# Two more u tiles in each head of the PEER ranking, and more gathered dots beside them

## The chip, the cores and the metric

One core of one Trainium2 chip runs the whole kernel. The metric is device microseconds for one execution; lower is better. Three runs of the kernel before gave 2048.4, 2052.14 and 2053.71 us, median 2052.14.

## The reference, cut to what matters

The kernel computes a hybrid encoder block for 512 positions of width 1024 (16 meta tokens and 512 frames go in; the last layer norm is on 512). Input norm, one combined projection, a sparse attention branch, a recurrent branch, output projection and norm come first and are not touched. The change lies in the last part, a product-key retrieval of single-neuron experts:

```python
q = (xf @ wq).reshape(n, 8, 2, 128)
s = einsum('nhpd,hpkd->nhpk', q, subkeys)          # 8 heads, 2 halves, 128 keys
s_top, i_top = top_k(s, 16)
best_s, best_j = top_k(all 16 x 16 sums of pairs, 16)
expert = key1 * 128 + key2;  gate = softmax(best_s)
h = einsum('nd,nhkd->nhk', xb, u[expert])
coef = gate * gelu(h)
out = einsum('nhk,nhkd->nd', coef, v[expert])      # u, v: 16384 x 1024
```

Each position picks 8 x 16 = 128 of 16384 experts.

## The kernel before, in words

**Two ways through the experts.** For 384 positions (`DENSE`) the kernel computes densely: all 16384 experts in 128 tiles of 128, each a *u tile* (u times the activations, then gelu) and a *sum* (weighted coefficients times v). For the first 128 positions it gathers: GpSimd issues an indirect DMA for each of the 128 picks of u rows and then of v rows (`gather_rows`, L1542), and VectorE does a dot with the u row (`dot_rows`, L1552) or adds the weighted v row (`add_rows`, L1561). Eight slots (`GATHER_RING`) hold gathered rows; the gather of number n waits until dot n - 8 is done.

**A weight tile.** Weights are split into a high and a low part in float32r. The SyncE queue loads a 512 KB tile into `w_staged`, ScalarE writes its high part (L1833, L1868), GpSimd (L1804) or from the lots on VectorE (L2173) writes the low part as the difference. TensorE multiplies 16 times with the high part (L1934) and then, after a wait for the low part, 8 times with the low part (L1938). Four slots hold split weights, so ScalarE and the low part run at most three to four tiles ahead of TensorE. ScalarE applies the gelu to the finished tile (L1839) and sends it to HBM (`parked_gelu`, a *parked* tile, 192 KB), from where it is loaded in the sums.

**The stages.**
- *Ranking*, 8 heads. Each head has 6 weight tiles: two query tiles (512 positions), then four u tiles (384 positions); the scores against the subkeys (L1948) stand ahead of the second u tile. ScalarE copies the scores behind that second u tile's gelu (L1860), and VectorE ranks them (`rank`, L2065 to L2119): maxima, indexes and replacements on 128 keys, a cast of the indexes (L2085), sums of pairs (L2086), the same on 256 candidates, then the lookup of the picked keys (L2092 to L2114) and `pick_index` (L2119). Behind the rank of head h VectorE does the dots of head h - 1 (`DOTS_A_HEAD`, 3). GpSimd makes the low parts in order; behind the last one of head h + 1 it waits for the index of head h and issues that head's gathers, in one block.
- *Between*, 16 u tiles. VectorE makes the gate softmax; ScalarE does its exponential behind tile 9 of them, and TensorE transposes picks and gates ahead of tile 12 (`GATES_AT`), for which it waits.
- *Lots*, 24 of 16 positions each. The gates are spread into dense form by one-hot matmuls (L1992), with two u tiles, two gathers and two dots in each lot. SyncE stores 1 MB for each lot, and issues two weight loads with it.
- *Behind the lots*, 6 u tiles with one dot each. GpSimd issues the gathers freely from here on, and already in the lots.
- *Sums*, 128 of them, L2019. For the first 102 (`PARKED`) the gelu is loaded; for the other 26 (`FRESH`) a u tile is computed two experts ahead. VectorE weighs with the gates (L2200), splits the coefficients (L2204), makes the low parts, and does the rest of the dots and adds in step (`used_by`): 1.1 for each parked expert, then about 3 for each fresh one.

Each engine's order is written out by hand in its own block; semaphores count tiles. The host lays `stream` out in the order in which the tiles are used.

Of the kernel before, what the change touches and what calls it, by code (L numbers as in the profile page):

```python
# [41 lines left out]
EXPERT_KEYS, PEER_HEADS, PEER_TOPK = 128, 8, 16  # L42
LOT = 16
PICKS = PEER_HEADS * PEER_TOPK

DENSE = SEQ - P
LOTS = DENSE // LOT
BETWEEN = 16
PARKED = 4 * PEER_HEADS + BETWEEN + 2 * LOTS + 6
GATHER_RING = 8  # L50
MARK, FILL, LOW = -3.4e38, -3.3e38, -1.0e30

# [64 lines left out]
def build(nc, a, out):  # L117

    with ExitStack() as ctx:
# [20 lines left out]
        gates_dram = nc.dram_tensor("branch_gates", [2 * KD, P, SEQ], F32, kind="Internal").ap()  # L140
        parked = nc.dram_tensor("parked_gelu", [PARKED, P, DENSE], F32, kind="Internal").ap()

# [1422 lines left out]
def peer(nc, a, g, out):  # L1565
# [3 lines left out]
    h_tok, gathering, eps = g["h_tok"], g["gathering"], g["eps"]  # L1569
    NP = PEER_HEADS * PEER_TOPK  # L1570
    K = PEER_TOPK
    PER_HEAD = 6
    QUERIES = 2 * PEER_HEADS
    TOPK_TILES = PEER_HEADS * PER_HEAD
    FIRST_LOT = TOPK_TILES + BETWEEN
# [6 lines left out]
    RING = 4  # L1582
    BY_POOL = FIRST_LOT
    DEEP = 2 * RING
    LOOP, COEFS, HLS = 8, 4, 3
    TILES_D = DENSE // P
    FRESH = EXPERT_KEYS - PARKED
    LEAD = 2

    V_AT, U_AT, s = {}, {}, QUERIES + PARKED  # L1590
    for k in range(EXPERT_KEYS):
        if k + LEAD < EXPERT_KEYS and k + LEAD >= PARKED:
# [3 lines left out]
        s += 1  # L1596
    STREAMED = s

    BEHIND = PARKED - (4 * PEER_HEADS + BETWEEN + 2 * LOTS)
    DOTS_A_HEAD, DOTS_A_LOT, DOTS_BEHIND = 3, 2, 1  # L1600
    IN_LOTS = DOTS_A_HEAD * (PEER_HEADS - 1)
    used_behind = [IN_LOTS + DOTS_A_LOT * LOTS + DOTS_BEHIND * (n + 1) for n in range(BEHIND)]
    EARLY = used_behind[-1]
    A_PARKED = 1.1
    BEFORE_FRESH = EARLY + int(A_PARKED * PARKED)
    used_by = [EARLY + int(A_PARKED * (k + 1)) if k < PARKED else
               min(2 * PICKS, BEFORE_FRESH + -(-(2 * PICKS - BEFORE_FRESH) * (k + 1 - PARKED) // (FRESH - HLS)))
               for k in range(EXPERT_KEYS)]
    DOTTED = next(k for k in range(EXPERT_KEYS) if used_by[k] >= PICKS)
    used_by[DOTTED] = PICKS  # L1610

    def expert_of(s):

        return s // PER_HEAD * (PER_HEAD - 2) + (s % PER_HEAD - 2) if s < TOPK_TILES else s - QUERIES

    def place_of(s):

# [29 lines left out]
    with ExitStack() as ctx:  # L1647
# [53 lines left out]
        w_high, w_low, late_low = sem("w_high"), sem("w_low"), sem("late_low")  # L1701
        tile_done, gelu_made = sem("tile_done"), sem("gelu_made")
# [17 lines left out]
        tile_bank = lambda n, is_query: n % 2 if is_query else 2 + n % 2  # L1720
# [98 lines left out]
        def _(act):  # L1819
# [8 lines left out]
            def high(s, j, landings, free=True):  # L1828

                act.wait_ge(landed[j % RING], landings * 16)  # L1830
                if free:
                    act.wait_ge(tile_done, s - 2)
                nc.scalar.activation(w_hl[:, j % RING, 0, :], staged[:, j % RING, :], ACT.Copy).then_inc(w_high, 1)  # L1833

            def gelu(s, n, m, turn, bank):

                act.wait_ge(tile_done, s + 2)
                act.wait_ge(act_parked[m % 2], turn * 16)
                nc.scalar.activation(act_out[:, m % 2, 0:DENSE], ps[:, bank, 0:DENSE], ACT.Gelu).then_inc(gelu_made, 1)  # L1839
                act.wait_ge(gelu_made, n + 3)  # L1840
                nc.scalar.dma_start(parked[n], act_out[:, m % 2, 0:DENSE]).then_inc(act_parked[m % 2], 16)
# [4 lines left out]
            with act.Fori(0, PEER_HEADS // 2) as i:  # L1846
                for j in range(2 * PER_HEAD):
                    r, m = j // PER_HEAD, j % PER_HEAD
                    high(i * (2 * PER_HEAD) + (j + 3), j + 3, i * 3 + ((j + 3) // RING + 1))
                    if m < 2:  # L1850
                        act.wait_ge(tile_done, i * (2 * PER_HEAD) + (j + 2))
                        nc.scalar.activation(qT[:, m, :], ps[:, tile_bank(m, True), :], ACT.Copy).then_inc(q_copied, 1)
                        continue
                    n = 4 * r + m - 2
                    gelu(i * (2 * PER_HEAD) + j, i * 8 + n, n, i * 4 + (n // 2 + 1), tile_bank(n, False))
                    if m == 3:
                        act.wait_ge(topped, i * 2 + (r + 1))
                        for x in range(2):
                            act.wait_ge(s_done, i * 4 + (2 * r + x + 1))
                            nc.scalar.activation(s_head[:, r, x], ps[:, 4 + 2 * r + x, :].rearrange("p (t k) -> p t k", t=NT),  # L1860
                                                 ACT.Copy).then_inc(s_copied, 1)
# [25 lines left out]
            for n in range(LOTS):  # L1887
                if n >= 2:
                    act.wait_ge(lot_stored[n % 2], 16 * (n // 2))
                s = FIRST_LOT + TILES_A_LOT * n  # L1890
# [32 lines left out]
        def _(pe):  # L1923
            pe.sem_inc(tile_done, 1)

            def tile(s, j, bank, width, low, before):

                pe.wait_ge(w_high, s + 1)
                for x in before:
                    pe.wait_ge(*x)  # L1930
                lo = SEQ - width
                for k in range(KD):
                    for part in range(2):
                        nc.tensor.matmul(ps[:, bank, 0:width], w_hl[:, j % RING, 0, P * k:P * (k + 1)],  # L1934
                                         h_hl[:, part, k, lo:SEQ], start=(k == 0 and part == 0), stop=False)
# [19 lines left out]
            with pe.Fori(0, PEER_HEADS // 2) as i:  # L1955
                for j in range(2 * PER_HEAD):
                    r, m = j // PER_HEAD, j % PER_HEAD
                    s = i * (2 * PER_HEAD) + j
                    if m < 2:
                        tile(s, j, tile_bank(m, True), SEQ, (w_low, s + 1), [(q_copied, i * 4 + (2 * r + m + 1))])  # L1960
                        continue
                    if m == 3:
                        scores(i, r)
                    n = 4 * r + m - 2
                    tile(s, j, tile_bank(n, False), DENSE, (w_low, s + 1), [(gelu_made, i * 8 + (n + 1))])

            low_of = lambda s: (w_low, s + 1) if s < BY_POOL else (late_low, s - BY_POOL + 1)

# [293 lines left out]
def lay_out(v):  # L2262

    w = v["w_in"][0]
    A = HEADS * HD
    at = [0, A, A + KV, 2 * A + KV, 2 * A + KV + HD, 2 * A + KV + HD + HEADS]
    q, ckv, qi, ki, wi = (w[:, at[n]:at[n + 1]] for n in range(5))
    b = w[:, at[5]:at[5] + 3 * A + 256]
    gates = w[:, at[5] + 3 * A + 256:]
    cols = np.concatenate([qi, ki, ki, ckv, b, q, gates], axis=1)  # L2270

    def by_columns(w):

        return np.ascontiguousarray(w.reshape(KD, P, -1, P).transpose(2, 1, 0, 3).reshape(-1, P, KD * P))

    wi_w = np.ascontiguousarray(wi.reshape(KD, P, HEADS).transpose(1, 0, 2))

    def columns(x):
        return x.reshape(-1, P).T

    twice = lambda x: np.concatenate([x, x])

    wq, u = by_columns(v["peer_wq"][0]), by_columns(v["peer_u"][0].T)
    order = [t for h in range(PEER_HEADS) for t in (wq[2 * h], wq[2 * h + 1], *u[4 * h:4 * h + 4])]
    stream = np.concatenate([np.stack(order), u[4 * PEER_HEADS:]])
    named = {"ln_in_g": v["ln_in_g"], "ln_in_b": v["ln_in_b"], "mu": v["b_mu"][0], "b_gate": v["b_gate"][0],
             "kv_g": v["a_kv_norm_g"][0], "ki_g": twice(v["a_kidx_g"][0]), "ki_b": twice(v["a_kidx_b"][0]),
             "w0": v["b_w0"][0], "a0": v["b_a0"][0], "k_k": v["b_k_k"][0], "k_a": v["b_k_a"][0],
             "r_k": v["b_r_k"][0], "lnx_g": v["b_lnx_g"][0], "lnx_b": v["b_lnx_b"][0],
             "ln1_g": v["ln1_g"][0], "ln1_b": v["ln1_b"][0]}  # L2290
    params = np.ascontiguousarray(np.concatenate([columns(named[n]) for n, _ in PARAMS], axis=1))
    return {"x": v["x"], "meta": v["meta"], "w_in_t": by_columns(cols), "wi_w": wi_w, "params": params,
            "ln_in_g": v["ln_in_g"], "ln_in_b": v["ln_in_b"],
            "w2": v["b_w2"], "a2": v["b_a2"], "g2": v["b_g2"],
            "w_uk": np.ascontiguousarray(v["a_w_uk"][0].reshape(KV, PAIRS, P).transpose(2, 1, 0)),
            "w_pa": v["w_pa"], "w_pb": v["w_pb"], "w_o": v["w_o"], "ln1_g": v["ln1_g"][0], "ln1_b": v["ln1_b"][0],
            "ln2_g": v["ln2_g"][0], "ln2_b": v["ln2_b"][0],
            "stream": stream, "u_rows": v["peer_u"][0], "v": v["peer_v"].reshape(EXPERT_KEYS, P, D),
            "sub_keys": np.ascontiguousarray(v["peer_subkeys"][0].reshape(2 * PEER_HEADS, EXPERT_KEYS, P).transpose(2, 0, 1)),
            "w_uv": v["a_w_uv"][0].reshape(KV, HEADS * HD)}  # L2300
# [15 lines left out]
```

## Time and profile before

| | |
|---|---|
| median of 3 runs | 2052.14 us |
| profiled execution | 2059.33 us, span 2057.6 us |
| PE | 1920.2 us, 93% |
| PEld | 1625.3 us, 79% |
| DVE | 1509.3 us, 73% |
| ACT | 764.6 us, 37% |
| POOL | 604.0 us, 29% |
| mean granted TensorE clock | 0.954 |
| moved by DMA | 416.58 MB, mean 202 GB/s |

PE is TensorE, DVE is VectorE, ACT is ScalarE, POOL is GpSimd, SP is SyncE; PEld are TensorE's weight loads. The shares are of the span. The ranking lies at 763 to 1002 us of the span, the 16 tiles between up to about 1077, the lots up to 1351, the sums from 1385 on.

### The profile page before, as it was taken

The numbers are of one execution on the slowest core, as the hardware profiler recorded it, in microseconds if no ns is written. First come the engines' busy times: TensorE is split into PE (matmuls) and PEld (weight loads), VectorE is DVE, ScalarE is ACT, GpSimd is POOL, SyncE is SP. The second block draws the span as 40 slices with busy tenths as digits, with TensorE's granted clock in tenths as the row PEclk, the third lists the DMA queues.
The fourth block names the chain that finished last, engine by engine and source line by source line (L and its number), as shares of the span: only waits on it lengthen the run. The fifth ranks groups of instructions, "written<-read, shape, count | busy, mean of one in ns | idle before, by whom it ended". The sixth has DMA issues, their size and how long they took to land.

```text
span 2057.6 us, 33992 instructions
## 1 busy us (share of the span) xinstructions
PE 1920.2 (93%) x13250; PEld 1625.3 (79%) x13250; DVE 1509.3 (73%) x2841; ACT 764.6 (37%) x1113; POOL 604.0 (29%) x403
## 2 busy tenths in 40 slices
PE   5989998789989879999899999989999999999996
PEld 4978876348974349999899999977888878889995
DVE  6277994314536248999989999947788878878887
ACT  3222454542220033343346666533333333333332
POOL 2322344000000025575662222222222323234540
PEclk9988999896999989999999999999999999999998
DMA  3211232000004024565568888989999999989991
GB/s 126 72 62 42 93 107 77 1 14 30 4 25 182 0 104 157 178 200 163 183 233 300 316 317 311 323 291 350 349 368 356 345 354 360 359 304 315 340 328 62
DMA packets 173724, 416.58 MB, mean 202 GB/s; under 512 B 13952, under 2 KB 89216, under 8 KB 170384
## 3 DMA queue, kind: packets, MB, share of 16 engines
q1 hardware_dynamic: 119728, 256.16, 36.7%
q0 software_dynamic: 36864, 134.23, 18.0%
q10 hardware_dynamic: 16992, 24.26, 3.2%
q8 instruction: 95, 1.56, 0.3%
q14 instruction: 45, 0.37, 0.1%
HBM read 363.08 MB, written 51.51 MB: 201 GB/s over the span
## 4 chain that ended last, share of the span: by engine, by line
PE 46%; DVE 11%; DMA 4%; issue 1%; ACT 0%; POOL 0%; SPq 0%; ACTq 0%; DVEq 0%
PE ps L2019 23%; PE ps L1934 14%; PE ps L1938 7%; PE ps L1992 3%; DMA gates<-dense_gates 2%; DMA w_staged<-in_stream 1%; DVE gathered_rows L1552 1%; DMA coef<-parked_gelu 1%; DVE keys L2085 1%; DVE top_at L2068 1%; DVE top_at L2077 1%; DVE s_head L2071 1%; DVE best_at L2068 0%; DVE best_at L2077 0%; DVE cand L2071 0%
## 5 line engine op out<-in xcount | busy, mean ns | idle before, releaser
L2019 PE MATMUL ps<-w_hl,coef_hl 128*128 128x512 f32 x2304 | 544.7, 397 | 7.5 <-DVE coef_hl L2204 7.4
L2019 PEld LDWEIGHTS ps<-w_hl,coef_hl 128*128 128x128 f32 x2304 | 436.2, 190 | 109.1 <-DVE coef_hl L2204 9.4
L1934 PE MATMUL ps<-h_hl,w_hl 128*128 128x384 f32 (+1 forms) x2304 | 449.5, 347 | 15.3 <-DVE h_hl L2039 8.7
L1934 PEld LDWEIGHTS ps<-h_hl,w_hl 128*128 128x128 f32 x2304 | 408.9, 190 | 30.0 <-issue 9.1
L1542 POOL DMA_INDIRECT gathered_rows<-in_u_rows,pick_index x128 | 166.5, 1301 | 426.4 <-DVE pick_hidden L1552 346.2
L1542 POOL DMA_INDIRECT gathered_rows<-in_v,pick_index x128 | 161.8, 1264 | 278.5 <-DVE h_tok L1561 239.3
L1868 ACT ACTIVATE w_hl<-w_staged 128x1024 fp32r<-128x1024 f32 x143 | 152.0, 1063 | 243.2 <-PE ps L2019 155.1
L1938 PE MATMUL ps<-h_hl,w_hl 128*128 128x384 f32 (+1 forms) x1152 | 231.5, 342 | 6.8 <-POOL w_hl L1804 6.8
L1938 PEld LDWEIGHTS ps<-h_hl,w_hl 128*128 128x128 f32 x1152 | 204.3, 189 | 12.5 <-POOL w_hl L1804 7.5
L1804 POOL TENSOR_TENSOR w_hl<-w_staged,w_hl 128x1024 fp32r<-128x1024 f32 x64 | 159.7, 2515 | 50.1 <-ACT w_hl L1833 33.9
L2173 DVE TENSOR_TENSOR w_hl<-w_staged,w_hl 128x1024 fp32r<-128x1024 f32 x130 | 157.9, 1219 | 18.4 <-ACT w_hl L1868 18.4
L632 PE MATMUL ps<-hT_hl,w_hl 128*128 128x264 f32 (+1 forms) x1024 | 168.1, 323 | 0.0
L1561 DVE SCALAR_TENSOR_TENSOR h_tok<-gathered_rows,pick_hidden,h_tok 128x1024 f32<-128x1024 f32 x128 | 163.9, 1281 | 5.5
L297 POOL TENSOR_TENSOR w_hl<-w_staged,w_hl 128x1024 fp32r<-128x1024 f32 x40 | 102.9, 2572 | 213.4 <-ACT w_hl L480 213.4
L632 PEld LDWEIGHTS ps<-hT_hl,w_hl 128*128 128x128 f32 x1024 | 150.6, 198 | 14.4 <-issue 2.8
L1552 DVE CUSTOM_DVE_ANT_0 gathered_rows<-gathered_rows,h_tok 128x1024 f32<-128x1024 f32 x128 | 155.1, 1237 | 0.0
L1868 ACT ACTIVATE w_hl<-h1T 128x1024 fp32r<-128x1024 f32 x78 | 83.0, 1064 | 190.8 <-PE ps L2019 144.6
L1799 POOL IOTA count<- 128x1024 bf16 x1 | 1.1, 1072 | 401.8 <-POOLq L111 401.8
L2204 DVE TENSOR_TENSOR coef_hl<-coef,coef_hl 128x384 fp32r<-128x384 f32 x128 | 71.1, 556 | 64.9 <-ACT coef_hl L1904 64.4
L2200 DVE TENSOR_TENSOR coef<-coef,gates 128x384 f32<-128x384 f32 x128 | 71.4, 558 | 57.0 <-ACT coef L1910 32.4
L1839 ACT ACTIVATE h1T<-ps 128x384 f32<-128x384 f32 x102 | 50.1, 491 | 163.9 <-PE ps L1938 163.9
L1883 ACT ACTIVATE lot<-ps 128x512 f32<-128x512 f32 x96 | 96.4, 1111 | 19.9 <-PE ps L1992 18.7
(316 smaller groups left out, 2518.9 us busy)
## 6 DMA issues: line engine op xcount, KB each, us to landing
w_staged<-in_stream SPq DMA_DIRECT2D x132, 512.0 KB, 5.5
h1T<-in_v SPq DMA_DIRECT2D x66, 512.0 KB, 7.7
w_staged<-in_v SPq DMA_DIRECT2D x62, 512.0 KB, 7.2
dense_gates<-lot SPq DMA_DIRECT2D x24, 1024.0 KB, 4.9
gates<-dense_gates SPq DMA_DIRECT2D x16, 1536.0 KB, 14.3
w_staged<-in_w_in_t SPq DMA_DIRECT2D x40, 512.0 KB, 3.4
parked_gelu<-h1T ACTq DMA_DIRECT2D x102, 192.0 KB, 4.0
coef<-parked_gelu SPq DMA_DIRECT2D x102, 192.0 KB, 6.4
```

Of the source, the lines that this page charges most:

```text
L297: nc.gpsimd.tensor_tensor(w_hl[:, j, 1, :], w_staged[:, j, :], w_hl[:, j, 0, :].bitcast(F32), ALU.subtract).then_inc(w_low, 1)
L632: nc.tensor.matmul(banks[b], w_hl[:, j, 0, P * k:P * (k + 1)], hT_hl[:, part, k, lo:hi], start=(k == 0 and part == 0), stop=False)
L1542: nc.gpsimd.indirect_dma_start(gathering["rows"][:, slot, :], None, table, bass.IndirectOffsetOnAxis(gathering["index"][:, column:column + ...
L1552: nc.vector.tensor_tensor_reduce(rows, rows, h_tok[:, 0, :], 1.0, 0.0, ALU.mult, ALU.add, gathering["hidden"][:, n:n + 1]).then_inc(gather ...
L1561: nc.vector.scalar_tensor_tensor(h_tok[:, 0, :], gathering["rows"][:, slot, :], gathering["hidden"][:, pick:pick + 1], h_tok[:, 0, :], ALU ...
L1804: nc.gpsimd.tensor_tensor(w_hl[:, j % RING, 1, :], staged[:, j % RING, :], w_hl[:, j % RING, 0, :].bitcast(F32), ALU.subtract).then_inc(w_ ...
L1868: nc.scalar.activation(w_hl[:, s % RING, 0, :], stage[place_of(s)], ACT.Copy).then_inc(w_high, 1)
L1883: nc.scalar.activation(lot[:, n % 2, :, FOUR * q:FOUR * (q + 1)].rearrange("p k n -> p n k"), ps[:, 4 + q, :].rearrange("p (n k) -> p n k" ...
L1934: nc.tensor.matmul(ps[:, bank, 0:width], w_hl[:, j % RING, 0, P * k:P * (k + 1)], h_hl[:, part, k, lo:SEQ], start=(k == 0 and part == 0), ...
L1938: last = nc.tensor.matmul(ps[:, bank, 0:width], w_hl[:, j % RING, 1, P * k:P * (k + 1)], h_hl[:, 0, k, lo:SEQ], start=False, stop=(k == KD ...
L2019: last = nc.tensor.matmul(ps[:, 2 + 2 * t + half, :], coef_hl[:, k % HLS, c, P * t:P * (t + 1)], w_hl[:, s % RING, v, 512 * half:512 * (ha ...
L2173: v_.tensor_tensor(w_hl[:, s % RING, 1, :], stage[place_of(s)], w_hl[:, s % RING, 0, :].bitcast(F32), ALU.subtract).then_inc(late_low, 1)
```

## The change

The constants change, and with them the places of the u tiles in the stream, in the order of each engine and in the semaphore counts. Each head of the ranking has 8 weight tiles, six of them u tiles (48 instead of 32 in all), and VectorE and GpSimd handle 8 gathered rows a head behind rank 0 to 6 (56 instead of 21). Twelve u tiles instead of 6 lie behind the lots, with a dot each. 124 tiles are parked instead of 102, and 4 instead of 26 are computed among the sums. The dots and adds that are left, 140 instead of 181, are spread evenly over the sums.

```diff
-PARKED = 4 * PEER_HEADS + BETWEEN + 2 * LOTS + 6
+EXPERTS_A_HEAD = 6
+PARKED = EXPERTS_A_HEAD * PEER_HEADS + BETWEEN + 2 * LOTS + 12
...
-    PER_HEAD = 6
+    PER_HEAD = EXPERTS_A_HEAD + 2
...
-    DOTS_A_HEAD, DOTS_A_LOT, DOTS_BEHIND = 3, 2, 1
+    DOTS_A_HEAD, DOTS_A_LOT, DOTS_BEHIND = 8, 2, 1
...
-    A_PARKED = 1.1
-    BEFORE_FRESH = EARLY + int(A_PARKED * PARKED)
-    used_by = [EARLY + int(A_PARKED * (k + 1)) if k < PARKED else
-               min(2 * PICKS, BEFORE_FRESH + -(-(2 * PICKS - BEFORE_FRESH) * (k + 1 - PARKED) // (FRESH - HLS)))
-               for k in range(EXPERT_KEYS)]
+    used_by = [min(2 * PICKS, EARLY + -(-(2 * PICKS - EARLY) * (k + 1) // (EXPERT_KEYS - HLS))) for k in range(EXPERT_KEYS)]
...
-        return s // PER_HEAD * (PER_HEAD - 2) + (s % PER_HEAD - 2) if s < TOPK_TILES else s - QUERIES
+        return s // PER_HEAD * EXPERTS_A_HEAD + (s % PER_HEAD - 2) if s < TOPK_TILES else s - QUERIES
...
-                    high(i * (2 * PER_HEAD) + (j + 3), j + 3, i * 3 + ((j + 3) // RING + 1))
+                    high(i * (2 * PER_HEAD) + (j + 3), j + 3, i * (2 * PER_HEAD // RING) + ((j + 3) // RING + 1))
...
-                    n = 4 * r + m - 2
-                    gelu(i * (2 * PER_HEAD) + j, i * 8 + n, n, i * 4 + (n // 2 + 1), tile_bank(n, False))
+                    n = EXPERTS_A_HEAD * r + m - 2
+                    gelu(i * (2 * PER_HEAD) + j, i * (2 * EXPERTS_A_HEAD) + n, n, i * EXPERTS_A_HEAD + (n // 2 + 1),
+                         tile_bank(n, False))
...
-    order = [t for h in range(PEER_HEADS) for t in (wq[2 * h], wq[2 * h + 1], *u[4 * h:4 * h + 4])]
+    order = [t for h in range(PEER_HEADS) for t in (wq[2 * h], wq[2 * h + 1], *u[EXPERTS_A_HEAD * h:EXPERTS_A_HEAD * (h + 1)])]
```

## Rows read from the trace of the kernel before

**Rows 1.** Windows: stretch, length, busy us of each engine, PEclk, DMA share, GB/s.
```profile
1500.00:1540.00 40.00, 40.00 (x174) 32.42 (x173) 33.10 (x52) 13.40 (x18) 11.44 (x11) 1.00 1.00 365
...
1660.00:1700.00 40.00, 38.50 (x166) 30.89 (x165) 34.31 (x41) 13.93 (x19) 11.25 (x10) 1.00 1.00 355
```

**Rows 2.** Timeline of TensorE: start us, us, what, [idle before <-releaser].
```profile
824.27 3.83 PE L1934 MATMUL ps<-h_hl,w_hl 128*128 128x512 f32 x16
...
845.33 2.93 PE L1934 MATMUL ps<-h_hl,w_hl 128*128 128x384 f32 x16
...
853.65 3.83 PE L1934 MATMUL ps<-h_hl,w_hl 128*128 128x512 f32 x16
...
976.36 2.11 PE L1938 MATMUL ps<-h_hl,w_hl 128*128 128x512 f32 x8 [1.36 <-POOL w_hl L1804]
...
1010.58 2.93 PE L1938 MATMUL ps<-h_hl,w_hl 128*128 128x384 f32 x8 [5.43 <-POOL w_hl L1804]
...
1367.75 5.26 PE L1934 MATMUL ps<-h_hl,w_hl 128*128 128x384 f32 x16 [3.90 <-ACT h1T L1839]
...
1411.48 13.70 PE L2019 MATMUL ps<-w_hl,coef_hl 128*128 128x512 f32 x47 [3.77 <-DVE coef_hl L2204]
```

**Rows 3.** Chain that ended last, 960 to 1070: start us, us, what.
```profile
1002.94 1.69 POOL gathered_rows L1542
...
1010.58 2.93 PE ps L1938 x8
```

**Rows 4.** Timeline of VectorE, the rank of one head.
```profile
845.42 1.22 DVE L1552 CUSTOM_DVE_ANT_0 gathered_rows<-gathered_rows,h_tok 128x1024 f32<-128x1024 f32 x1
...
848.86 1.64 DVE L2065 MAX8 top<-s_head 128x8 f32<-128x128 f32 x8
...
858.98 1.65 DVE L2085 CAST keys<-top_at 128x128 bf16<-128x128 uint32 x1
860.55 1.21 DVE L2086 TENSOR_TENSOR cand<-top 128x1024 f32<-128x1024 f32 x1
...
874.92 0.17 DVE L2119 SCALAR_TENSOR_TENSOR pick_index<-picks 128x16 uint32<-128x16 f32 x1
```

**Rows 5.** Timeline of GpSimd in the ranking.
```profile
847.78 1.97 POOL L1542 DMA_INDIRECT gathered_rows<-in_u_rows,pick_index  x1 [0.31 <-issue]
850.05 0.94 POOL L1542 DMA_INDIRECT gathered_rows<-in_u_rows,pick_index  x1 [0.30 <-issue]
851.00 9.49 POOL L1804 TENSOR_TENSOR w_hl<-w_staged,w_hl 128x1024 fp32r<-128x1024 f32 x4
...
973.94 14.14 POOL L1804 TENSOR_TENSOR w_hl<-w_staged,w_hl 128x1024 fp32r<-128x1024 f32 x6
1002.94 1.69 POOL L1542 DMA_INDIRECT gathered_rows<-in_u_rows,pick_index  x1 [14.86 <-DVE pick_index L2119]
...
1008.16 11.72 POOL L1804 TENSOR_TENSOR w_hl<-w_staged,w_hl 128x1024 fp32r<-128x1024 f32 x5
```

**Rows 6.** Timeline of GpSimd, first and last of eight gathers in a row.
```profile
1064.36 1.09 POOL L1542 DMA_INDIRECT gathered_rows<-in_u_rows,pick_index  x1
...
1075.15 1.23 POOL L1542 DMA_INDIRECT gathered_rows<-in_u_rows,pick_index  x1 [0.30 <-issue]
```

**Rows 7.** Timeline of ScalarE.
```profile
847.68 1.06 ACT L1833 ACTIVATE w_hl<-w_staged 128x1024 fp32r<-128x1024 f32 x1
```

**Rows 8.** Timeline of VectorE, later operations beside low parts.
```profile
981.92 6.28 DVE L2085 CAST keys<-top_at 128x128 bf16<-128x128 uint32 x1
...
1016.15 3.88 DVE L2085 CAST keys<-top_at 128x128 bf16<-128x128 uint32 x1
...
1040.25 0.17 DVE L2119 SCALAR_TENSOR_TENSOR pick_index<-picks 128x16 uint32<-128x16 f32 x1
...
1041.48 3.41 DVE L1552 CUSTOM_DVE_ANT_0 gathered_rows<-gathered_rows,h_tok 128x1024 f32<-128x1024 f32 x1
```

**Rows 9.** Chain that ended last, at the last lot.
```profile
1355.93 10.22 DMA w_staged<-in_stream
```

More of the change, by code:

```diff
@@ L1597, in peer @@
     STREAMED = s
-    BEHIND = PARKED - (4 * PEER_HEADS + BETWEEN + 2 * LOTS)
-    DOTS_A_HEAD, DOTS_A_LOT, DOTS_BEHIND = 3, 2, 1
+    BEHIND = PARKED - (EXPERTS_A_HEAD * PEER_HEADS + BETWEEN + 2 * LOTS)
+    DOTS_A_HEAD, DOTS_A_LOT, DOTS_BEHIND = 8, 2, 1
     IN_LOTS = DOTS_A_HEAD * (PEER_HEADS - 1)
@@ L1963, in _ @@
                         scores(i, r)
-                    n = 4 * r + m - 2
-                    tile(s, j, tile_bank(n, False), DENSE, (w_low, s + 1), [(gelu_made, i * 8 + (n + 1))])
+                    n = EXPERTS_A_HEAD * r + m - 2
+                    tile(s, j, tile_bank(n, False), DENSE, (w_low, s + 1), [(gelu_made, i * (2 * EXPERTS_A_HEAD) + (n + 1))])
             low_of = lambda s: (w_low, s + 1) if s < BY_POOL else (late_low, s - BY_POOL + 1)
@@ L2283, in lay_out @@
     wq, u = by_columns(v["peer_wq"][0]), by_columns(v["peer_u"][0].T)
-    order = [t for h in range(PEER_HEADS) for t in (wq[2 * h], wq[2 * h + 1], *u[4 * h:4 * h + 4])]
-    stream = np.concatenate([np.stack(order), u[4 * PEER_HEADS:]])
+    order = [t for h in range(PEER_HEADS) for t in (wq[2 * h], wq[2 * h + 1], *u[EXPERTS_A_HEAD * h:EXPERTS_A_HEAD * (h + 1)])]
+    stream = np.concatenate([np.stack(order), u[EXPERTS_A_HEAD * PEER_HEADS:]])
     named = {"ln_in_g": v["ln_in_g"], "ln_in_b": v["ln_in_b"], "mu": v["b_mu"][0], "b_gate": v["b_gate"][0],
```

## The prediction

> **What bounds the kernel now.** I read the windows by stage first. From the ranking to the end TensorE is busy for all of nearly every window, the mixed sums included (40.00 of 40 us at 1500 to 1540), where the DMA engines are also at a share of 1.00 [rows 1]. The same number of weight tiles goes through TensorE before and after, so moving 22 u tiles from the sums to earlier places moves TensorE time and removes none. Only TensorE's holes can be won or lost. The timeline of TensorE shows where they are: two in the ranking, 1.36 us before 976.36 and 5.43 us before 1010.58, and those behind the lots, 3.90 us before 1367.75 and 3.77 us before 1411.48 [rows 2]. The chain of work that ended last runs in the ranking through VectorE's ranks, GpSimd's gathers and GpSimd's low parts into the matmuls that waited [rows 3]. So GpSimd and VectorE in the ranking decide.
>
> **The budget of one head.** TensorE starts a head at 824.27 and the next at 853.65: 29.38 us for two query tiles, four u tiles and the scores [rows 2]. A u tile is 24 matmuls. Of the 29.38 us, two query tiles take 5.45 each and the scores 1.7, which leaves 4.16 for a u tile. A head of the new kernel is 29.38 + 2 x 4.16 = 37.7 us.
>
> VectorE's rank goes from 848.86 to 875.01, then come the dots [rows 4]. It has four parts: 10.1 us of maxima and indexes up to the cast at 858.98; the cast; 14.5 us from 860.55 to the index at 874.92; the dots, three from 845.42 to 848.86, 1.15 each. The cast took 1.65 us, but it ended at 860.63, just after GpSimd's four low parts (851.00 + 9.49 = 860.49) [rows 4, 5]; unheld I take 0.3. With eight dots (9.2 us) a head costs VectorE 10.1 + 0.3 + 14.5 + 9.2 = 34.1 us. That would fit in 37.7.
>
> GpSimd needs eight low parts at 2.37 (19.0 us) and eight gathers. Beside dots a gather took 1.70 and 1.97 plus 0.3 between, behind them 0.94 [rows 5]; eight in a row took 1064.36 to 1076.38, 12.0 us [rows 6]. About four of the new eight run beside dots at 2.1 and four at 1.25: 13.4 us. Together 32.4 of 37.7.
>
> **What does not fit: the order.** GpSimd runs its gathers in one block after the last low part of a head, and each later low part waits behind it. A low part can't run more than four tiles ahead, the depth of the ring. In the new head the last tile's high part comes behind the gelu of the fourth tile and the score copies. In this place of a head the fourth tile ended at 845.33 and the high part at 847.68 + 1.06 [rows 2, 7]; with 2.4 us of low part that is 5.8 us after the fourth tile. TensorE needs the next low part after four more u tiles and the first 16 matmuls of a query tile (3.83 at 853.65, of which 3.7 until the next may start [rows 2]): 20.3 us after it. A block of 13.4 and a low part of 2.4 end at 21.6. So the lead, of which three gathers left some 8 us, is gone: 1.3 us lost if nobody else is late (0 with 12.0 us of gathers), and every wait for an index is now TensorE's.
>
> Second, low parts keep VectorE out. The cast at 981.92 took 6.28 us and ended at 988.20, when GpSimd's six low parts (973.94 + 14.14 = 988.08) ended; the cast at 1016.15 ended at 1020.03, after five (1008.16 + 11.72 = 1019.88); a dot at 1041.48 took 3.41 instead of the 1.22 at 845.42 [rows 4, 5, 8]. In the first case it passed over ends of low parts without being let in. The maxima and indexes ran beside the same bursts at their usual length [rows 4]. The Trainium skill ("SBUF — State Buffer", on engine and DMA ports) has an exclusive lock between VectorE's operations of two SBUF inputs and GpSimd, held for one whole instruction by whoever started first. The trace agrees that there is such a wait, but shows it reaching to the end of a burst of several instructions.
>
> Before, GpSimd idled for its index while VectorE ran the last third of a rank, so little met: the wait before the gather at 1002.94 is 14.86 us [rows 5]. After, let P be the end of an index. Gathers P + 1.5 to P + 14.9 (the first needs the ring slot of the first dot, since eight gathers fill the ring). Burst of low parts: four are waiting and a fifth comes in time, as at 1008.16, 11.7 us, to P + 26.6. Dots to P + 9.2, maxima to P + 19.3; the cast wants to start there and is held 7.3 us to P + 26.6. Then 0.3 + 14.5 gives P + 41.4, and one later low part of 2.4 falls into the last 5 us of the rank: the next index at P + 43.7. Bounds: 34.1 (nothing held, then TensorE's 37.7 rules) and 46 (burst of six, 14.1). I take 43.7, because burst and cast are both placed by rows of this stage. That is 6.0 us a head over 37.7.
>
> It doesn't start at once. In the first heads the index is ahead of its gathers by some 6 us and more; I book 0.5 us for each of the first two blocks, 5 for the third, 6.0 for the four that follow. Ranking: 1 + 5 + 24 = **+30 us** (bounds 1 and 43).
>
> **After the ranking.** The gate softmax must be done when TensorE has twelve more tiles. From the last block's P: TensorE resumes at P + 17.3, ends the waiting tile by P + 19.9 and eleven more at P + 65.7. VectorE: cast done at P + 26.9, then 20.4 us, as from 1020.03 to the index at 1040.25 + 0.17 with a low part every 4.16 us [rows 8]: P + 47.3. Eight dots there: the one of 3.41 lost 2.2 to a low part [rows 8], and about four low parts fall into their time, so eight take 9.2 + 4 x 2.2 = 18: P + 65.3. Small copy, subtraction, ScalarE's table load and exponential, sum, reciprocal and a product follow, each small; with one more held by a low part I put 6 on them: gates at P + 71.3. TensorE waits 5.6, and its clock costs it about 1.5 more after a hole (at 1010.58 eight matmuls took 2.93 [rows 2]; a third of a u tile's 4.16 is 1.39): **+7** (0 to 12).
>
> **What goes.** The two holes of before, 1.36 + 5.43, and 1.9 of slow matmuls behind the second (1.5 in the first eight, an estimated 0.4 in the next tile): **-8.7**.
>
> **Lots, and the twelve tiles behind them.** Same TensorE work for each lot, same two dots and gathers: 0. The last loads are issued in pairs behind each lot's copies; the chain shows the pair of 1355.93 in flight for 10.22 us, beside the last lot's 1 MB store, ahead of the hole before 1367.75 [rows 2, 9]. This is the same after. Six further tiles follow with one load each, 4.16 us apart; per tile load, gather and parked write are 0.52 + 0.52 + 0.20 MB, 299 GB/s, under the 355 and 365 of [rows 1]. The first gates and parked tiles then no longer crowd those loads. Bounds -6 (holes of 3.90 and before it, filled) and +3; I take 0. What hides it is the four tiles of lead; if the loads took over 12 us, each would show.
>
> **The sums.** The parked part grows from 102 to 124 experts. Per expert of 4.18 us: 0.524 (v) + 0.197 (parked) + 0.197 (gates, an eighth) + gathers of 0.524. Before 1.1 gathers, 358 GB/s; after (256 - 116)/125 = 1.12, 360. Rows show 365 at 1500 to 1540 with TensorE full, and one loss of 1.5 us at 1660 to 1700 [rows 1]. VectorE was busy 33.10 of 40 there, with the same work for an expert. I take **+1.5**, one more such loss in a stretch longer by a fifth (0 to +7: if 355 GB/s were the limit, 1.4% of 124 x 4.18 = 518 us).
>
> **Sum.** 30 + 7 - 8.7 + 1.5 = +29.8. Against the profiled execution (2059.33 us around a span of 2057.6) that is 2089; it lay 7.2 above the median of 2052.14, so the forecast for the median is **2082 us**. Its own range, from 41 to 45 us a head and 0 to 12 behind, is 2064 to 2098.
>
> **Rivals.**
> *Faster: the ranking stays TensorE's.* VectorE needs 34.1 unheld, GpSimd 32.4. If low parts fall beside maxima (18 us a head) and the indexes keep ahead, a head is 37.7 to 38.5 and the holes of before go: -8.7 + 0 to 5, and up to -6 behind the lots, 2040 to 2049, say 2045. For it: the cast at 858.98 was held for little over 1 us. Against: for no place of the block does my table give a cycle under 40, since a burst ends either over the cast or over the last third.
> *A held operation waits for one low part only.* Then the cast costs 2.4, the operation behind it 2.4, the last third 2.4: 34.1 + 7.2 = 41.3, 3.6 a head: 4 x 3.6 + 4 = 18, 5 behind, 2068. This is what the skill's rule (the same page) would make of it. Against: the 6.28 us.
> *Much slower.* Gathers at 2.1 us throughout (17 us) and bursts of six: index to index 50 us, 12 a head, +60 in the ranking, or bursts of six in every head (46 us) with the sums starved for 7: 2096 to 2120.
> *The edit isn't what it says:* the stream's order, the expert numbers and the semaphore counts change together, so I see no such case.
>
> **Chances.** Forecast 0.50, faster rival 0.20, one low part only 0.18, much slower 0.12. Within 0.3% of before (2046 to 2058, what a measurement of this kernel can tell) lies a third of the faster rival and some of the third: 0.10. Faster 0.17, slower 0.73. Range 2044 to 2104.
>
> **What would show it.** Casts of over 5 us in most heads that end with a burst of low parts; index to index about 44 us; holes of 4 to 6 us in TensorE at the first query tile of heads 3 to 7, ended by GpSimd; a hole before the transposes. It is wrong if heads take 38 us, or if the holes sit in the sums and end with a DMA.

## The result and the profile after

The changed kernel takes 2086.53 us (median of 4, 2085.67 to 2087.67) against 2052.93 (median of 4 by then): a ratio of 1.0168, 95% interval 1.0151 to 1.0186. The profiled execution took 2086.8 us, its span 2084.8. The forecast was 2082, +30; measured is +33.6.

The front of the kernel, which no run here changed, ended at a different place in nearly each profile: TensorE's first matmul of the ranking started at 762.74 before, at 756.03 after, and at 754 to 768 in the other runs. So lengths are counted below from that matmul to the end of the span, each from one profile: 1294.9 us before, 1328.8 after, +33.9. They divide as follows, each stretch measured between the same two matmuls of both traces, with the moved tiles taken off at 4.16 us each:

| stretch | before | after | tiles moved | left | forecast |
|---|---|---|---|---|---|
| ranking, to the second tile behind it | 250.6 | 343.9 | +66.6 | +26.8 | 30 - 8.7 = +21.3 |
| from there to the transposes | 46.2 | 48.9 | 0 | +2.7 | +7 |
| to the first sum | 325.3 | 347.3 | +25.0 | -3.0 | 0 |
| sums, to the last three | 642.1 | 558.0 | -91.5 | +7.4 | +1.5 |
| the rest | 30.6 | 30.6 | 0 | 0 | 0 |

TensorE's timeline after the change (the columns of [rows 2]):

```profile
921.31 3.78 PE L1936 MATMUL ps<-h_hl,w_hl 128*128 128x512 f32 x8 [7.72 <-POOL w_hl L1801]
...
965.62 3.15 PE L1936 MATMUL ps<-h_hl,w_hl 128*128 128x512 f32 x8 [4.38 <-POOL w_hl L1801]
...
1009.15 3.78 PE L1936 MATMUL ps<-h_hl,w_hl 128*128 128x512 f32 x8 [3.92 <-POOL w_hl L1801]
...
1053.87 3.78 PE L1936 MATMUL ps<-h_hl,w_hl 128*128 128x512 f32 x8 [4.38 <-POOL w_hl L1801]
...
1097.23 2.93 PE L1936 MATMUL ps<-h_hl,w_hl 128*128 128x384 f32 x8 [4.08 <-POOL w_hl L1801]
...
1148.83 1.18 PE L1977 MATMUL ps<-ident,picks 128*128 128x128 f32 x9 [1.58 <-DVE picks L2137]
...
1455.02 4.35 PE L1932 MATMUL ps<-h_hl,w_hl 128*128 128x384 f32 x16 [4.20 <-ACT h1T L1836]
...
1526.03 94.14 PE L2017 MATMUL ps<-w_hl,coef_hl 128*128 128x512 f32 x397 [6.04 <-DVE coef_hl L2202]
```

The two holes of the ranking [rows 2] have become five, four at the first tile of a head and the last at the first tile behind the ranking, all ended by GpSimd's low part. Behind the first four the eight matmuls take 3.15 to 3.78 us, where a third of a query tile's 5.45 is 1.8. These slow matmuls count too: in the first stretch of the table TensorE stood still for 24.5 us after against 6.8 before, +17.7, and its matmuls, without the moved tiles, took 9.1 us more (mean granted clock 0.95 in this stretch, 0.98 before).

Five smaller holes lie late in the sums:

```profile
1842.68 33.73 PE L2017 MATMUL ps<-w_hl,coef_hl 128*128 128x512 f32 x144 [1.05 <-DVE coef_hl L2202]
1877.61 33.73 PE L2017 MATMUL ps<-w_hl,coef_hl 128*128 128x512 f32 x144 [1.20 <-DVE coef_hl L2202]
1912.96 33.73 PE L2017 MATMUL ps<-w_hl,coef_hl 128*128 128x512 f32 x144 [1.61 <-DVE coef_hl L2202]
1947.51 33.73 PE L2017 MATMUL ps<-w_hl,coef_hl 128*128 128x512 f32 x144 [0.82 <-DVE coef_hl L2202]
1982.97 42.09 PE L2017 MATMUL ps<-w_hl,coef_hl 128*128 128x512 f32 x180 [1.73 <-DVE coef_hl L2202]
```

GpSimd's timeline of one head after:

```profile
944.25 2.84 POOL L1801 TENSOR_TENSOR w_hl<-w_staged,w_hl 128x1024 fp32r<-128x1024 f32 x1 [3.23 <-ACT w_hl L1830]
950.15 1.20 POOL L1543 DMA_INDIRECT gathered_rows<-in_u_rows,pick_index  x1 [3.06 <-DVE pick_hidden L1553]
951.65 1.97 POOL L1543 DMA_INDIRECT gathered_rows<-in_u_rows,pick_index  x1 [0.30 <-issue]
...
962.25 0.94 POOL L1543 DMA_INDIRECT gathered_rows<-in_u_rows,pick_index  x1 [0.30 <-issue]
963.20 11.73 POOL L1801 TENSOR_TENSOR w_hl<-w_staged,w_hl 128x1024 fp32r<-128x1024 f32 x5
```

and VectorE's in the same head, from the index of one head to the next, then two later indexes:

```profile
948.06 0.17 DVE L2117 SCALAR_TENSOR_TENSOR pick_index<-picks 128x16 uint32<-128x16 f32 x1
...
957.32 1.64 DVE L2063 MAX8 top<-s_head 128x8 f32<-128x128 f32 x8
...
967.45 7.62 DVE L2083 CAST keys<-top_at 128x128 bf16<-128x128 uint32 x1
...
991.60 0.17 DVE L2117 SCALAR_TENSOR_TENSOR pick_index<-picks 128x16 uint32<-128x16 f32 x1
...
1036.32 0.18 DVE L2117 SCALAR_TENSOR_TENSOR pick_index<-picks 128x16 uint32<-128x16 f32 x1
...
1079.68 0.17 DVE L2117 SCALAR_TENSOR_TENSOR pick_index<-picks 128x16 uint32<-128x16 f32 x1
```

These rows show the cycle of the prediction. With P, the end of the index, at 948.2, the gathers run from P + 1.9 to P + 15.0 (forecast 1.5 and 14.9), the burst of five low parts ends at 974.93, P + 26.7 (26.6), the cast wants to start at P + 19.2 (19.3) and ends at 975.07, P + 26.8. From index to index it is 43.5, 44.7 and 43.4 us (43.7). In the first cast of the ranking that met a burst, earlier than I had expected one, the hold was longer:

```profile
876.03 9.02 DVE L2083 CAST keys<-top_at 128x128 bf16<-128x128 uint32 x1
884.98 3.42 DVE L2084 TENSOR_TENSOR cand<-top 128x1024 f32<-128x1024 f32 x1
```

```profile
873.12 14.20 POOL L1801 TENSOR_TENSOR w_hl<-w_staged,w_hl 128x1024 fp32r<-128x1024 f32 x6
```

This cast ended at 885.05, ahead of the burst's end at 887.32: it passed the ends of three low parts, was let in behind the fifth (884.89 is the sixth's start), and the sixth then held the addition that follows.

VectorE in the 16 tiles behind the ranking, which the prediction put at the index at P + 47.3 and the gates at P + 71.3, with P now 1079.85:

```profile
1127.33 0.17 DVE L2117 SCALAR_TENSOR_TENSOR pick_index<-picks 128x16 uint32<-128x16 f32 x1
...
1129.71 3.42 DVE L1553 CUSTOM_DVE_ANT_0 gathered_rows<-gathered_rows,h_tok 128x1024 f32<-128x1024 f32 x1
...
1145.88 2.81 DVE L2137 TENSOR_TENSOR picks<-picks,small 128x512 f32<-128x512 f32 x1
```

The index came at P + 47.6, the gates at P + 68.8.

Windows of the sums after (the columns of [rows 1]):

```profile
1740.00:1780.00 40.00, 40.00 (x174) 32.43 (x173) 33.50 (x40) 14.44 (x20) 12.28 (x11) 1.00 1.02 367
...
1900.00:1940.00 40.00, 38.39 (x165) 30.82 (x164) 31.40 (x38) 13.78 (x19) 11.26 (x10) 1.00 1.03 356
```

and the waits from 1500 us on (engine, line, waited for, us in total, times, longest):

```profile
DVE coef L2198 <- DMA gates<-dense_gates: 28.7, 13, 4.5
PEld ps L2017 <- DVE coef_hl L2202: 18.0, 8, 6.5
```

### The profile page after: what moved, and what is told of

It reads as the page before. It is cut to its first block, busy times and chain, and to the rows that moved or that the text cites. A ratio compares the mean times of both kernels' runs of the same rounds, so it can differ in the third digit from the quotient of the medians.

```text
span 2084.8 us, 34178 instructions
## 1 busy us (share of the span) xinstructions
PE 1922.1 (92%) x13250; PEld 1627.7 (78%) x13250; DVE 1544.5 (74%) x2825; ACT 764.8 (37%) x1113; POOL 633.0 (30%) x419
## 4 chain that ended last, share of the span: by engine, by line
PE 38%; DVE 18%; DMA 6%; issue 1%; ACT 0%; SPq 0%; ACTq 0%; DVEq 0%
PE ps L2017 19%; PE ps L1932 11%; PE ps L1936 5%; DMA gates<-dense_gates 4%; DVE gathered_rows L1553 3%; PE ps L1990 3%; DVE keys L2083 2%; DMA coef<-parked_gelu 1%; DVE is_place L2110 1%; DVE top_at L2075 1%; DVE top_at L2066 1%; DVE s_head L2069 1%; DVE best_at L2075 1%; DVE best_at L2066 1%; DVE cand L2069 1%
## 5 line engine op out<-in xcount | busy, mean ns | idle before, releaser
L1932 PE MATMUL ps<-h_hl,w_hl 128*128 128x384 f32 (+1 forms) x2304 | 451.0, 347 | 13.6 <-DVE h_hl L2037 8.7
L1936 PE MATMUL ps<-h_hl,w_hl 128*128 128x384 f32 (+1 forms) x1152 | 238.0, 348 | 24.5 <-POOL w_hl L1801 24.5
L1543 POOL DMA_INDIRECT gathered_rows<-in_v,pick_index x128 | 149.9, 1171 | 345.3 <-DVE h_tok L1562 310.2
L1936 PEld LDWEIGHTS ps<-h_hl,w_hl 128*128 128x128 f32 x1152 | 207.7, 192 | 32.7 <-POOL w_hl L1801 26.8
L1801 POOL TENSOR_TENSOR w_hl<-w_staged,w_hl 128x1024 fp32r<-128x1024 f32 x80 | 199.0, 2506 | 97.4 <-ACT w_hl L1830 78.8
L1866 ACT ACTIVATE w_hl<-w_staged 128x1024 fp32r<-128x1024 f32 x137 | 145.6, 1062 | 216.4 <-PE ps L2017 163.5
L2171 DVE TENSOR_TENSOR w_hl<-w_staged,w_hl 128x1024 fp32r<-128x1024 f32 x124 | 151.0, 1218 | 28.7 <-ACT w_hl L1866 28.7
L298 POOL TENSOR_TENSOR w_hl<-w_staged,w_hl 128x1024 fp32r<-128x1024 f32 x40 | 102.8, 2571 | 214.6 <-ACT w_hl L481 214.6
L1553 DVE CUSTOM_DVE_ANT_0 gathered_rows<-gathered_rows,h_tok 128x1024 f32<-128x1024 f32 x128 | 161.4, 1304 | 0.0
L1836 ACT ACTIVATE h1T<-ps 128x384 f32<-128x384 f32 x124 | 60.9, 491 | 208.0 <-PE ps L1936 207.9
L1866 ACT ACTIVATE w_hl<-h1T 128x1024 fp32r<-128x1024 f32 x68 | 72.3, 1064 | 162.9 <-PE ps L2017 150.6
```

The lines of the kernel that those rows point to most:

```text
L298: nc.gpsimd.tensor_tensor(w_hl[:, j, 1, :], w_staged[:, j, :], w_hl[:, j, 0, :].bitcast(F32), ALU.subtract).then_inc(w_low, 1)
L1543: nc.gpsimd.indirect_dma_start(gathering["rows"][:, slot, :], None, table, bass.IndirectOffsetOnAxis(gathering["index"][:, column:column + ...
L1553: nc.vector.tensor_tensor_reduce(rows, rows, h_tok[:, 0, :], 1.0, 0.0, ALU.mult, ALU.add, gathering["hidden"][:, n:n + 1]).then_inc(gather ...
L1801: nc.gpsimd.tensor_tensor(w_hl[:, j % RING, 1, :], staged[:, j % RING, :], w_hl[:, j % RING, 0, :].bitcast(F32), ALU.subtract).then_inc(w_ ...
L1866: nc.scalar.activation(w_hl[:, s % RING, 0, :], stage[place_of(s)], ACT.Copy).then_inc(w_high, 1)
L2171: v_.tensor_tensor(w_hl[:, s % RING, 1, :], stage[place_of(s)], w_hl[:, s % RING, 0, :].bitcast(F32), ALU.subtract).then_inc(late_low, 1)
```

## Experiments

Times are medians; ratios are to the kernel before, run on the same chip. "Touched part" is the length from the first ranking matmul in the run's profile.

### The dots left out

```diff
-                        dot_rows(nc, dve, h_tok, gathering, n)
+                        dve.wait_ge(gathering["landed"][n % GATHER_RING], 16 * (n // GATHER_RING + 1))
+                        v_.tensor_copy(gathering["hidden"][:, n:n + 1],
+                                       gathering["rows"][:, n % GATHER_RING, 0:1]).then_inc(gathering["used"], 1)
```

> The 56 dots of the ranking are left out (VectorE only copies one column for each, so those hidden values are wrong); gathers, their block and all else stay. Theory A (VectorE's cycle: 24.9 us of rank, 9.2 of dots and 7 to 9 us of being held by GpSimd's burst of low parts is what bounds a head at 44 us): without the dots the cycle is under 37.7 us, gather blocks start 37.7 us apart, the holes at the first query tile go, about 2054 us. Rival B (the block of eight gathers, which takes the low parts' lead, makes the holes): blocks stay as long, so holes of 2 to 4 us stay in each head, over 2070 us.

Measured 2049.98 us, ratio 0.9989 (0.9965 to 1.0013); touched part 1289.6, 39 less than after. The ranking has no hole. VectorE there:

```profile
1021.47 0.27 DVE L2083 CAST keys<-top_at 128x128 bf16<-128x128 uint32 x1
...
1046.00 0.17 DVE L2117 SCALAR_TENSOR_TENSOR pick_index<-picks 128x16 uint32<-128x16 f32 x1
...
1059.16 0.28 DVE L2083 CAST keys<-top_at 128x128 bf16<-128x128 uint32 x1
```

The casts are 37.7 us apart, TensorE's head, and take 0.27 when nothing holds them (I had taken 0.3). This agrees with theory A. It doesn't exclude rival B by itself: without dots beside it the block is shorter, 10.0 us (1014.88 to 1024.93) instead of 13.1, and by the prediction's sums a block of up to 12 us costs nothing. The next run keeps the dots and parts the block.

### Gathers in pairs

```diff
-                if 0 <= h < PEER_HEADS - 1 and m == PER_HEAD - 1:
-                    pool.wait_ge(gathering["picked"], h + 1)
-                    for n in range(DOTS_A_HEAD * h, DOTS_A_HEAD * (h + 1)):
+                h, m = divmod(s - (2 * PER_HEAD - 1), PER_HEAD)
+                first, end = {0: (0, 2), 1: (2, 4), 2: (4, 6), 3: (6, 8)}.get(m, (0, 0))
+                if 0 <= h < PEER_HEADS - 1 and end:
+                    pool.wait_ge(gathering["picked"], h + 1)
+                    for n in range(DOTS_A_HEAD * h + first, DOTS_A_HEAD * h + end):
```

> The eight gathers of a head are issued in pairs behind four successive low parts instead of in one block. Theory A: the cycle of VectorE stays the bound; dots are now held by the low parts between the pairs, and the last low parts run one behind the other when the cast comes, so index to index 44 to 50 us and 2086 to 2105 us. Rival B: no low part waits for more than two gathers, so the lead of the low parts is kept and the holes go: head 37.7 us, about 2054 us.

Measured 2092.02 us, ratio 1.0227 (1.0185 to 1.0269); touched part 1330.2. It is no cure. GpSimd and VectorE in one head:

```profile
959.32 0.94 POOL L1543 DMA_INDIRECT gathered_rows<-in_u_rows,pick_index  x1 [0.30 <-issue]
960.28 11.79 POOL L1801 TENSOR_TENSOR w_hl<-w_staged,w_hl 128x1024 fp32r<-128x1024 f32 x5
```

```profile
959.92 12.28 DVE L2084 CAST keys<-top_at 128x128 bf16<-128x128 uint32 x1
...
986.49 0.17 DVE L2118 SCALAR_TENSOR_TENSOR pick_index<-picks 128x16 uint32<-128x16 f32 x1
...
1032.19 0.18 DVE L2118 SCALAR_TENSOR_TENSOR pick_index<-picks 128x16 uint32<-128x16 f32 x1
```

The burst of five ended at 972.07 and the cast at 972.20: it waited past four ends of low parts. It had begun 0.36 us before the burst, beside the gather of 959.32, and needs 0.27 when nothing holds it, so this gather didn't let it through either. The next index comes 45.7 us later; over the last four heads it is 45.7 to 48.2. With no block of more than two gathers the holes are still there (8.76, 5.48 and 9.37 us), so neither the length of the block nor the lead is the bound.

### Two blocks of four

```diff
-                first, end = {0: (0, 2), 1: (2, 4), 2: (4, 6), 3: (6, 8)}.get(m, (0, 0))
+                first, end = {0: (0, 4), 5: (4, 8)}.get(m, (0, 0))
```

> The eight gathers in two blocks of four, the second five low parts later. Theory A: the first block ends at P + 9.9, the burst of five low parts at P + 21.8, beside the maxima; the cast is held 2.5 us instead of 7.5 and some low parts hold the last third: index to index 39 to 41 us, holes of 1 to 3 us, about 2064 us. Rival B: a block of four fits into the lead, no holes, about 2054 us. If the hold did not depend on where the burst lies: 44 us, 2086 us.

Measured 2064.10 us, ratio 1.0075 (1.0050 to 1.0101); touched part 1304.7. Same work, other order, 22 us less than the one block:

```profile
954.49 11.82 POOL L1801 TENSOR_TENSOR w_hl<-w_staged,w_hl 128x1024 fp32r<-128x1024 f32 x5
966.46 1.94 POOL L1543 DMA_INDIRECT gathered_rows<-in_u_rows,pick_index  x1 [0.16 <-issue]
```

```profile
963.72 2.72 DVE L2084 CAST keys<-top_at 128x128 bf16<-128x128 uint32 x1
...
983.96 0.18 DVE L2118 SCALAR_TENSOR_TENSOR pick_index<-picks 128x16 uint32<-128x16 f32 x1
...
1023.56 0.17 DVE L2118 SCALAR_TENSOR_TENSOR pick_index<-picks 128x16 uint32<-128x16 f32 x1
```

Here the burst lies beside the maxima, the cast is held 2.45 us, and the index comes every 39.6 us.

### Gates loaded earlier

```diff
-                if k % LOOP == LOOP - 3 and LOOP < k < EXPERT_KEYS - LOOP:
+                if k % LOOP == LOOP - 5 and LOOP < k < EXPERT_KEYS - LOOP:
```

> Each load of gates in the sums is issued two experts (8.4 us) earlier. Theory: the five holes of 0.8 to 1.7 us from 1842 to 1983 are loads of gates that are issued three experts ahead and take 16 us; two experts more remove them: 2080 to 2081 us. Rival: the DMA engines are at their limit there and whatever is loaded comes late, so the holes move to other loads: 2085 to 2088 us.

Measured 2084.25 us (1.0127 to 1.0200 to before), touched part 1324.0, 4.8 less than after. All five holes of the later sums are gone, and no wait for gates is left. The theory holds; the 4.8 us fall a little short of the holes' 6.4, since a hole behind the lots was longer in this run (5.86).

### Each half of the change alone

```diff
-EXPERTS_A_HEAD = 6
+EXPERTS_A_HEAD = 4
```

> Only the dots: eight gathered dots a head, but four u tiles (12 tiles behind the lots, 108 parked). Theory A: the cycle does not depend on TensorE's tiles, index to index stays 42 to 44 us against 29.4 us of TensorE, holes of 12 to 14 us in each head, 2130 to 2150 us. Rival C (the longer heads with their eight low parts make the cycle): index to index 36 to 38 us, 2095 to 2110 us.

```diff
-    DOTS_A_HEAD, DOTS_A_LOT, DOTS_BEHIND = 8, 2, 1
+    DOTS_A_HEAD, DOTS_A_LOT, DOTS_BEHIND = 3, 2, 1
```

> Only the tiles: six u tiles a head, 12 behind the lots, but three gathered dots a head. Theory A: VectorE's cycle is 24.9 + 3.4 + at most 9 of being held, under 37.7, so the ranking has no hole, 1 to 3 us less after the softmax. The 35 dots and gathers go to the sums: 1.4 a parked expert, 395 GB/s wanted where up to 367 was shown, so DMA should stretch 518 us of sums by 6 to 8%, 30 to 42 us with holes that end with DMA: 2075 to 2090 us. Rival (the DMA engines have more to give than any row shows): 2043 to 2050 us.

The dots alone: 2133.48 us, ratio 1.0402 (1.0361 to 1.0443), two runs. VectorE from index to index:

```profile
1019.51 0.17 DVE L2117 SCALAR_TENSOR_TENSOR pick_index<-picks 128x16 uint32<-128x16 f32 x1
...
1038.89 7.58 DVE L2083 CAST keys<-top_at 128x128 bf16<-128x128 uint32 x1
...
1060.76 0.18 DVE L2117 SCALAR_TENSOR_TENSOR pick_index<-picks 128x16 uint32<-128x16 f32 x1
```

GpSimd's burst beside that cast:

```profile
1034.65 11.68 POOL L1801 TENSOR_TENSOR w_hl<-w_staged,w_hl 128x1024 fp32r<-128x1024 f32 x5
```

The index comes every 41.25 us, with the same hold of the cast; TensorE needs 29.4 and has holes of 8.7 to 13.8. The cycle is VectorE's own. It is 0.75 under my range; the difference to the 43.4 to 44.7 of the whole change lies behind the cast: from its end to the end of the index it is 14.5 us here, with one low part beside it, and 16.5 to 17.9 there, with three.

The tiles alone: 2085.67 us, ratio 1.0169 (1.0127 to 1.0210), two runs: as slow as the whole change, and for another reason. The ranking has no hole. The sums have a dozen; two windows and the wait behind them:

```profile
1580.00:1620.00 40.00, 39.12 (x169) 31.42 (x168) 36.16 (x58) 14.57 (x20) 16.72 (x13) 1.00 1.05 388
...
1740.00:1780.00 40.00, 34.82 (x142) 27.83 (x142) 30.62 (x36) 11.98 (x16) 16.31 (x12) 0.91 0.96 331
```

```profile
DVE coef L2198 <- DMA gates<-dense_gates: 52.7, 13, 7.7
```

With 1.4 gathers an expert the sums ask for 395 GB/s and get 325 to 388. The time fits theory A, but the cause is not settled: the waits are for gates, which are issued three experts ahead here too, and whether they would go with a lead of five, as in the run above, was not run. The two halves don't pay for each other. The six u tiles do hide much of the dots' time, which costs 83 us without them, but the eight dots a head take the tiles' holes out of the sums and put about as much back into the ranking, so the whole change takes as long as its tiles alone.

### The kernel before with two dots a head

```diff
-    DOTS_A_HEAD, DOTS_A_LOT, DOTS_BEHIND = 3, 2, 1
+    DOTS_A_HEAD, DOTS_A_LOT, DOTS_BEHIND = 2, 2, 1
```

> The kernel before with two dots and gathers a head instead of three. Theory A: there VectorE's cycle (24.9 + 3.4 + being held, 31.8 to 34.3 at the end) against 29.4 of TensorE made the two holes of 1.36 and 5.43 us; with 1.15 us less a head it still lags by 1.3 to 3 us in the later heads, but reaches the lead's end later: one hole of 0 to 3 us instead of 6.8 plus 1.9 of slow clock, 2044 to 2049 us. Rival (the holes come from the block of three gathers alone, or TensorE's time is all that counts): 2052 us.

Measured 2049.54 us, ratio 0.9996 (0.9975 to 1.0018). In its profile the ranking has no hole and the touched part is 1283.6, 11 less than before, but the medians of 12 and 23 runs, in which the front varies, don't show a gain. About 9 of the 11 are the two holes with their slow matmuls. The trace shows that the holes go with one dot and one gather less a head; it doesn't tell the dot from the gather, and the gain in time isn't shown.

### Three cures, and the loads of v

`e5_together` has the two blocks, the early gates, and of the eight dots ahead of the softmax four behind it:

```diff
-                for n in range(DOTS_A_HEAD * (h - 1), DOTS_A_HEAD * h):
+                for n in range(DOTS_A_HEAD * (h - 1), DOTS_A_HEAD * h - (4 if h == PEER_HEADS - 1 else 0)):
...
+            for n in range(IN_LOTS - 4, IN_LOTS):
+                dot_rows(nc, dve, h_tok, gathering, n)
             low(BY_POOL)
```

> Three cures in one kernel: two blocks of four gathers, gates loaded two experts earlier, and of the eight dots ahead of the gate softmax four put behind the transposed gates. Theory A with its smaller terms: the ranking as with two blocks (index to index 39.6 us, holes of 1.3 to 1.6), the hole before the transposes (5.97 with two blocks) gone, no holes for gates: 2064 - 6 - 1.5 - 5 = about 2051 us, level with the kernel before. If VectorE's time before the softmax is not what makes the hole before the transposes, about 2059 us.

Measured 2053.87 us, ratio 1.0013 (0.9995 to 1.0031); touched part 1290.1. The hole before the transposes, 5.97 us with two blocks, is gone.

The next two move the first v loads, to settle the holes behind the lots:

```diff
-                if n == LOTS - 2:
-
-                    load_from(QUERIES + PARKED, QUERIES + PARKED + 3)
...
             load_from(FIRST_BEHIND + RING, QUERIES + PARKED)
+            load_from(QUERIES + PARKED, QUERIES + PARKED + 3)
```

> The kernel of e5 with the first three loads of v tiles behind the last loads of u tiles. Its holes behind the lots, 0.46 and 4.83 us with 1.7 of slow matmuls, go if these loads make them: from the first ranking matmul on 1290.1 - 7 = 1283 us, median about 2047 us. Rival (pairs of u loads): 1290, 2054 us.

Measured 2046.81 us, ratio 0.9984 (0.9968 to 0.9999); touched part 1281.6. No hole of over 0.2 us is left between the end of the ranking and the wait of 2.11 before the first sum: the three v loads ahead of the u loads in one queue made the holes of this kernel, not the pairs beside the store.

> The kernel before with two dots a head (as in e6), each load of gates two experts earlier, and the first three loads of v tiles behind the last loads of u tiles instead of ahead of the last two lots'. The holes of 0.3, 0.4, 2.0 and 2.1 us behind the lots (with 1.7 of slow matmuls) go if the three v loads are what delays the u loads, the four of 0.5 to 1.6 in the sums if late gates make them. From the first ranking matmul on, 1283.6 us in e6: about 1272 us; median about 2040 us. Rival (the hole behind the lots comes from the pairs of u loads themselves beside the lot's store): -4 for the gates alone, 1279 and 2046 us.

Measured 2039.65 us, ratio 0.9955 (0.9939 to 0.9972): 0.45% under the kernel before. Touched part 1276.6. The median is as forecast, but the touched part is 4.6 us over the 1272 of the theory and nearer to the rival's 1279. What is left are the holes around the first sums:

```profile
1347.58 4.58 PE L1932 MATMUL ps<-h_hl,w_hl 128*128 128x384 f32 x16 [2.15 <-ACT h1T L1837]
1365.27 22.95 PE L2017 MATMUL ps<-w_hl,coef_hl 128*128 128x512 f32 x90 [3.39 <-DVE coef_hl L2202]
1391.53 28.78 PE L2017 MATMUL ps<-w_hl,coef_hl 128*128 128x512 f32 x116 [3.32 <-DVE coef_hl L2202]
```

The first of them lies behind the lots and starts with ScalarE's wait for a u tile:

```profile
1346.00 1.06 ACT L1866 ACTIVATE w_hl<-w_staged 128x1024 fp32r<-128x1024 f32 x1 [8.36 <-DMA w_staged<-in_stream]
```

This load was issued at 1334.78, right behind the last lot's store and ahead of the v loads, and took 11.2 us. So in this kernel the v loads made three of the four holes behind the lots, and the rival, the pair beside the store, is not excluded for the fourth.

## Why the prediction was right, and where its terms were off

**No TensorE time is won by moving tiles.** Right: the same 7049 matmuls run in the touched part of both. TensorE was idle there for 38.8 us before and 65.5 after, +26.7, and busy for 1256.1 and 1263.3, +7.2: the slow matmuls behind the holes.

**VectorE's cycle bounds a head, by the order and not by the sum.** Right, and the deciding step. Unheld it needs 34.1 us of 37.7. (The budget's 4.16 for a u tile is 4.19 by its own subtraction; the plain tiles that were added do take 4.16, so 37.7 stands.) The runs show the cycle: without the dots 37.7 a head; with the gathers in pairs 45.7 to 48.2; in two blocks 39.6; with TensorE's head at 29.4 still 41.25. The rival in which low parts fall beside maxima by themselves fell with the one block, and came half true when the block was cut to place them there.

**A held operation waits for the whole burst.** Right for each cast from the fourth head on, but no strict rule. In five places of these traces a cast was let in one low part early: at 876.03 after the change and at the same place of the run with early gates, at 918.17 before (it ended at 919.81, the burst at 922.10), at 1008.01 with the gathers in pairs and at 831.71 with the dots alone. What let it in there is not known. The rival of one low part only would have made the cycle 41.3, and the cast past four ends of low parts in the run with pairs excludes it.

**The block takes the lead.** Overrated. It decides only how soon a late index reaches TensorE: with the dots kept and the block parted in pairs the holes stayed. What a block of the full 13.1 us costs when no index is late, 1.3 us by the prediction, no run shows, since without dots it lasted 10.0.

**The start of the ranking, +1 and +5.** Undersized together: +0.2 and +9.95. The third block's hole was 7.72 us, with slow matmuls behind it. The rank before it met the burst of six, which held a cast and the addition behind it, 9.02 and 3.42 us, so it took 51.5 from index to index, where I had counted 43.7. With 6.3 instead of 6.0 us for each later head this is most of the 5.5 us by which the ranking's +21.3 fell short.

**Behind the ranking, +7.** Oversized by 4.3: three low parts instead of four met the dots, and after two slow tiles TensorE came to the transposes at P + 67.4 instead of 65.7. The hole was 1.58.

**Lots and tiles behind them, 0.** -3.0, within the bounds. I blamed the pairs of u loads beside the lot's store, on the strength of one row [rows 9]; moving the v loads took all holes there out of the changed kernel with its cures, and three of four out of the kernel before.

**The sums, +1.5.** Mis-sized: +7.4. My term looked at rates, which were right (366 and 367 GB/s with TensorE full). The loss came from a lead in time: a load of gates is issued three experts ahead, in these traces some 13.7 us before it is wanted, and the five that made the holes took 15.9 to 17.4. Issued five ahead, the five holes, 6.4 us together, were gone. Before, the last 26 experts took 8.4 us each and gave such a load 23 us. That is not the whole answer: the parked experts before had the same short lead and only one such hole (1.50 us, [rows 1]), and what made the loads slower late in the sums after the change is not shown. Net of that hole the gates make 4.9 of the 7.4 us. The rest is at the first sums: holes of 1.56, 0.54 and 6.04 us against one of 3.77, less 1.7 us of faster matmuls. Their cause is left open.

That the forecast of +30 came so near to +33.6 is thus partly luck of signs: ranking and sums 11 us too low together, the softmax and the stretch to the sums 7 too high.

## What to carry to other kernels

Where GpSimd and VectorE work side by side, draw one cycle of both with its order, not their sums: an engine with a tenth of its time to spare was the bound because of where the other's back-to-back instructions lay, and changing only that order won back 22 us. When the pace of a loop changes, check every load that is issued a fixed number of iterations ahead. When work moves from one stage to another, the stage that takes it pays, so time each half of such a change by itself: here both halves were slower than the kernel before.

## What the hardware showed beyond expectation

A VectorE cast of 0.27 us took 12.28 us beside five GpSimd subtractions run back to back: at none of the ends between them was it let in; in five other places a cast was let in one subtraction before the last. The Trainium skill ("SBUF — State Buffer", section "SBUF: two separate sides") describes the lock for one instruction only. GpSimd's gathers didn't hold VectorE's dots (eight in 9.2 us beside them) but took 1.97 to 1.99 us instead of 0.94 there. For casts the traces differ: in the run without dots they took 0.27 beside gathers, in the run with pairs that of 959.92 was not through in the 0.36 us before the burst. The DMA engines moved 388 GB/s over 40 us in the run with the tiles alone, more than in any window of before or after.
